# A token mixer's projections computed as three products of fp32r parts, with the weights split on GpSimd, ScalarE and VectorE

## The reference, cut to what matters

```
x    = rmsnorm(h, final_norm)                 # end of block one
xn   = rmsnorm_2(x, g_mix)
proj = xn @ w_in
sb_q, sb_k, sb_v  (512 columns each)          # stick-breaking attention, 8 heads of 64
g_q, g_k, g_v     (512 each)                  # causal conv, silu, l2norm, gated delta rule
g_z (512), g_b, g_a (4 each)                  # output gate, beta and decay
gate_sb, gate_gdn (1024 each)                 # not touched by the change
o_sb = stick_breaking_attention(sb_q, sb_k, sb_v)
o_g  = gated_delta_rule(l2norm(q), l2norm(k), v, beta, g)
```

## Time and profile before

| | |
|---|---|
| runs of the kernel before | 1817.61, 1821.5, 1824.58 us; median 1821.5 us |
| span of the profiled execution | 1818.7 us, mean granted TensorE clock 0.960 |
| busy share in that span | PE 91%, DVE 59%, ACT 31%, POOL 19% |
| two norms, from the last down projection's end to L584 | about 696.6 to 705.6 us |
| sb_v and the first projection | 711.2 to 732 us |
| four rounds | 732.8 to 789.2 us |
| channels, g_b, g_a, g_z | 789.2 to 834.1 us |
| norm sums and reciprocal | 834.1 to 851.6 us |

### The profile page before, as it was taken

One profiled execution on the slowest core, in us unless ns is written; L12 is line 12 of the kernel. 1 busy time (PEld: TensorE's weight loads), 2 busy tenths in 40 slices (PEclk: granted clock), 3 DMA queues, 4 the chain that ended last, 5 costly groups with the idle time before them and its releaser, 6 DMA issues.

```text
span 1818.7 us, 22755 instructions
## 1 busy us (share of the span) xinstructions
PE 1647.0 (91%) x7883; PEld 1171.8 (64%) x7883; DVE 1072.1 (59%) x2454; ACT 566.0 (31%) x1111; POOL 348.4 (19%) x296
## 2 busy tenths in 40 slices
PE   7999999999999998999999999798797788888877
PEld 5888999868689995884664796444343344434333
DVE  6556555546455553546444642777777777666765
ACT  2544444335344441424110431122221222222222
POOL 3550000000000000000000000454434444443540
PEclk9999999999999998999999999799999989998989
DMA  6635566323466652522405340899999999999997
GB/s 210 187 93 162 170 187 198 133 61 99 153 181 186 198 153 67 162 95 92 185 24 185 139 151 27 353 420 421 421 421 422 421 421 421 421 421 421 422 420 297
DMA packets 205769, 437.43 MB, mean 241 GB/s; under 512 B 10608, under 2 KB 136976, under 8 KB 171792
## 3 DMA queue, kind: packets, MB, share of 16 engines
q0 software_dynamic: 36864, 268.45, 35.5%
q1 hardware_dynamic: 168848, 168.20, 28.8%
HBM read 435.54 MB, written 1.05 MB: 240 GB/s over the span
## 4 chain that ended last, share of the span: by engine, by line
PE 71%; DMA 16%; DVE 8%; issue 3%; ACT 1%; SPq 0%; POOL 0%; DVEq 0%; another core or an unknown queue 0%; ACTq 0%
PE ps L553 33%; DMA OT<-in_peer_uv,IX 13%; PE ps L1438 13%; PE ps L745 6%; PE ps L1229 3%; PE ps L1086 3%; PE ps L1099 3%; PE ps L720 2%; PE ps L584 2%; DMA SLOT<-in_peer_uv,IX 2%; DVE SLOT L2761 2%; PE ps L559 1%; PE ps L629 1%; DMA SLOT<-in_fox_w_in 1%; PE ps L1178 1%
## 5 line engine op out<-in xcount | busy, mean ns | idle before, releaser
L1944 POOL DMA_INDIRECT SLOT<-in_peer_uv,IX x128 | 138.5, 1082 | 1272.3 <-DVE IX L2755 1025.2
L1438 PE MATMUL ps<-SLOT,AR 128*128 128x512 f32 x512 | 267.2, 679 | 92.9 <-ACT AR L1862 92.9
L553 PE MATMUL ps<-ARH 128*128 128x256 f32 (+1 forms) x2248 | 298.8, 285 | 0.0
L553 PEld LDWEIGHTS ps<-ARH 128*128 128x128 f32 x2248 | 285.1, 191 | 3.8 <-issue 0.5
L1438 PEld LDWEIGHTS ps<-SLOT,AR 128*128 128x128 f32 x512 | 109.5, 219 | 244.2 <-issue 131.4
L2761 DVE SCALAR_TENSOR_TENSOR SLOT<-SLOT,V 128x1024 f32<-128x1024 f32 x128 | 153.1, 1224 | 74.5 <-DMA SLOT<-in_peer_uv,IX 72.5
L2078 DVE TENSOR_TENSOR ARH<-SLOT,ARH 128x2048 fp32r<-128x2048 f32 (+1 forms) x88 | 154.1, 1756 | 50.9 <-ACT ARH L1521 34.1
L1438 PE MATMUL ps<-AR 128*128 128x512 f32 x320 | 144.2, 600 | 8.3 <-ACT AR L1862 8.3
L1856 ACT ACTIVATE AR<-AR 128x4 f32<-128x4 f32 (+1 forms) x66 | 13.6, 205 | 370.4 <-DVE SLOT L2761 184.5
L745 PE MATMUL ps<-ARH 128*128 128x512 f32 x528 | 123.8, 390 | 0.0
L1438 PEld LDWEIGHTS ps<-AR 128*128 128x128 f32 x320 | 60.3, 192 | 81.8 <-issue 64.7
(11 more groups left out here) (424 smaller groups left out, 2611.1 us busy)
## 6 DMA issues: line engine op xcount, KB each, us to landing
SLOT<-in_w_gate SPq DMA_DIRECT2D x44, 512.0 KB, 4.0
SLOT<-in_w_up SPq DMA_DIRECT2D x44, 512.0 KB, 5.3
SLOT<-in_w_down SPq DMA_DIRECT2D x44, 512.0 KB, 5.2
SLOT<-in_w_in SPq DMA_DIRECT2D x9, 2048.0 KB, 8.2
SLOT<-in_fox_w_in SPq DMA_DIRECT2D x16, 512.0 KB
SLOT<-in_w_ckv SPq DMA_DIRECT2D x4, 2048.0 KB, 8.7
XT<-in_w_pq_by_head SPq DMA_DIRECT2D x8, 1024.0 KB
SLOT<-in_w_uq_by_pair SPq DMA_DIRECT2D x8, 768.0 KB, 4.8
```

Source lines behind the costliest of these rows:

```text
L553: m = pe.matmul(outp, l, r, start=(n_ == 0), stop=(n_ == len(pairs) - 1))
L1438: m = pe.matmul(ps[:, b, :], DIAG[:, j, :], v_row(j)[:, c * 512:(c + 1) * 512], start=False, stop=closing)
L1944: pool.indirect_dma_start(PAIR[j], None, pairs, bass.IndirectOffsetOnAxis(IX[:, t, j:j + 1], 0)).then_inc(gathered[j], 16)
```

## The change

All products of `xn` with the first 3592 columns of `w_in` (all but the gates) become three fp32r matmuls. XT is kept as two parts: ACT writes the high part from PSUM (`high_norm`), DVE the low part (`low_norm`), as the feed-forward layer does. The weights are split before use:

- sb_v (now SLOT0): POOL casts and subtracts, in four quarters of two chunks each, from the moment at which the weights are there, which is during the end of `ffn(1)`. The high parts go to OTR and the upper half of SLOT1.
- the four query and key pairs (SLOT1 and SLOT2 in turn): POOL casts the high part (`sb_pair_high`, 128 x 2048), DVE subtracts (`sb_low`, 128 x 2048). The first is placed on DVE ahead of the copy of sb_v, the second behind it, the third and fourth in rounds 0 and 1, between `sb_keep` and `sb_tail`.
- the three channel tiles (slots 3, 0, 3): ACT casts halves of 128 x 2048 (`mix_columns`), POOL subtracts (`mix_low`). ACT's casts stand in rounds 1 to 3, and, for the last tile, between the copies of the second and third channel piece.
- g_b, g_a: ACT casts, POOL subtracts, both small. g_z: ACT casts two halves after the fourth channel piece, POOL subtracts two halves; PE waits for both.
- the gates' projections still use a whole XT: POOL adds the two parts (128 x 2048) once PE has started on the work after g_z (`projected`, `xt_whole`).

The loop over rounds is written out on PE, ACT and DVE. The flush of two tiny matmuls after the first projection is gone. The SP list is reordered to match. The core of the diff:

```diff
@@ PE
-            turned(H, KC)
-            pe.wait_ge(here[2], T.next(here[2], 16))
+            turned(H, KC, reader="a")
             for t in range(NT):
                 take(6 + t)
-                grown_group(ps[:, 6 + t, :], [[(cols(XT, t, k), slot(2, KC, 512)[:, k, :])] for k in range(KC)]).then_inc(full["v"][6 + t], 1)
+                for k in range(KC):
+                    if t == 0 and k % 2 == 0:
+                        evacuated(k // 2)
+                        pe.wait_ge(mix_split[0], T.next(mix_split[0]))
+                    w = (sb_high(k), low_of(0, KC, 512)[:, k, :])
+                    for n_, (l, r) in enumerate(thirds(lambda h: cols(XHL[h], t, k), lambda h: w[h])):
...
+            def sb_proj(i):
+                p = 1 + i % 2
+                pe.wait_ge(mix_split[p], T.next(mix_split[p]))
+                take(0)
+                w = (HIGH[i % 2], low_of(p, 2, KC, P))
+                for s_ in range(2):
+                    m = group(ps[:, 0, s_ * S:(s_ + 1) * S], sum((thirds(lambda h: w[h][:, s_, k, :], lambda h: XHL[h][:, k, :]) for k in range(KC)), []))
...
             def channels(s_, g, b):
+                pe.wait_ge(mix_split[s_], T.next(mix_split[s_]))
...
+            pe.wait_ge(mix_split[2], T.next(mix_split[2], 2))
...
+            pending.append(sem("projected"))
...
+            pe.wait_ge(sem("xt_whole"), 1)
             for n_ in range(2):
                 gate_part(n_, n_)
@@ ACT
+            def mix_columns(s, g):
+                if g == 0:
+                    act.wait_ge(raw_here[s], T.next(raw_here[s], 16))
+                act.copy(columns(MIX_HIGH[s], g), columns(SLOT[s], g)).then_inc(sem("mix_high"), 1)
...
+            for i in range(3):
                 sb_soft()
                 qk_copy(0.125)
+                if i:
+                    mix_columns(3, i - 1)
                 sb_probs()
...
             sb_soft()
+            mix_columns(0, 0)
             sb_probs()
             ot_copy(2, 6)
+            mix_columns(0, 1)
             ot_copy(3, 6)
...
                 signal("pre_ready")
+                if n_ == 1:
+                    mix_columns(3, 0)
+                    mix_columns(3, 1)
...
+                if n_ == 3:
+                    act.wait_ge(raw_here[2], T.next(raw_here[2], 16))
+                    for q in range(2):
+                        act.copy(MIX_HIGH[2][:, 4 * q:4 * q + 4, :], chunks(SLOT[2], q)).then_inc(sem("mix_high"), 1)
@@ POOL
+            def mix_low(s, out_, raw, high):
+                pool.wait_ge(sem("mix_high"), T.next(sem("mix_high")))
+                pool.tensor_tensor(out_, raw, high.bitcast(F32), ALU.subtract).then_inc(mix_split[s], 1)
...
+            for q in range(4):
+                for k in (2 * q, 2 * q + 1):
+                    m = pool.tensor_copy(sb_high(k), view(SLOT[0][:], KC, 512)[:, k, :])
...
+                    m = pool.tensor_tensor(view(SLOTR[0][:], KC, 512)[:, k, :], view(SLOT[0][:], KC, 512)[:, k, :], sb_high(k).bitcast(F32), ALU.subtract)
+            pool.wait_ge(sem("ffn_over"), 1)
...
+            for i in range(PAIRS // 2):
+                sb_pair_high(i)
+            for s in (3, 0, 3):
+                for g in range(2):
+                    mix_low(s, columns(SLOTR[s], g), columns(SLOT[s], g), columns(MIX_HIGH[s], g))
+            mix_low(1, ...)
+            for q in range(2):
+                mix_low(2, chunks(SLOTR[2], q), chunks(SLOT[2], q), MIX_HIGH[2][:, 4 * q:4 * q + 4, :])
+            pool.wait_ge(sem("projected"), 1)
+            pool.tensor_tensor(XT[:], XTR[:].bitcast(F32), XT2R[:].bitcast(F32), ALU.add).then_inc(sem("xt_whole"), 1)
@@ DVE
             ffn(1)
+            signal("ffn_over")
...
-            norm("mix", squared=False)
+            scaled(H, D).then_inc(sem("xs_ready"), 1)
+            low_norm(XHL[1], XHL[0], "mix")
...
+            sb_low(0)
...
+            sb_low(1)
+            for i in range(PAIRS // 2):
                 sb_scores()
                 sb_keep()
+                if i < 2:
+                    sb_low(i + 2)
                 sb_tail()
@@ SP
+            projection(0, 1024)
+            sb_pair(0)
+            sb_pair(1)
+            projection(3, 1536)
+            projection(0, 2048)
+            sb_pair(2)
+            sb_pair(3)
+            fill(1, (slot(1, KC, 8), rows(w_in, 3584, 3592)), arrival=raw_here)
+            projection(2, 3072)
+            projection(3, 2560)
```

More of the change, by code:

```diff
@@ L653, in out_part @@
                     T.add(free["v"][6 + t])
-            def qk_part(s_):
-                if s_ == 0:
-                    take(0)
-                pe.wait_ge(here[s_], T.next(here[s_], 16))
-                m = group(ps[:, 0, s_ * S:(s_ + 1) * S], ((slot(s_, KC, P)[:, k, :], XT[:, k, :]) for k in range(KC)))
-                release(s_)
-                if s_ == 1:
-                    m.then_inc(full["a"][0], 1)
-                    T.add(free["a"][0])
-            def qk_proj():
-                qk_part(0)
-                qk_part(1)
             def flip(hh):
@@ L1023, in sb_turn @@
                 T.add(free["a"][6])
-            qk_proj()
+            sb_proj(0)
             evacuated(6, 7)
-            flush()
-            assert not pending
             sb_scores(0)
-            qk_proj()
+            sb_proj(1)
             sb_sums()
             sb_mix(0)
-            assert not pending
-            with T.loop("sb", 2) as i:
-                sb_scores(i + 1)
-                qk_proj()
+            for i in range(1, 3):
+                sb_scores(i)
+                sb_proj(i + 1)
                 sb_sums()
                 sb_turn()
-                sb_mix(i + 1)
-                assert not pending
+                sb_mix(i)
             def channels(s_, g, b):
+                pe.wait_ge(mix_split[s_], T.next(mix_split[s_]))
                 take(b)
+                w = (columns(MIX_HIGH[s_], g), columns(SLOTR[s_], g))
                 for c in range(2):
-                    m = group(ps[:, b, c * S:(c + 1) * S], ((slot(s_, KC, 512)[:, k, (2 * g + c) * P:(2 * g + c + 1) * P], XT[:, k, :])
-                                                             for k in range(KC)))
+                    m = group(ps[:, b, c * S:(c + 1) * S], sum((thirds(lambda h: w[h][:, k, c * P:(c + 1) * P], lambda h: XHL[h][:, k, :]) for k in range(KC)), []))
                 m.then_inc(full["a"][b], 1)
@@ L1052, in _ @@
             sb_scores(3)
-            pe.wait_ge(here[3], T.next(here[3], 16))
             channels(3, 0, 0)
@@ L1060, in _ @@
             sb_turn()
-            for n_, s_ in ((1, 2), (2, 3)):
-                pe.wait_ge(here[s_], T.next(here[s_], 16))
+            for n_, s_ in ((1, 0), (2, 3)):
                 for g in range(2):
@@ L1067, in _ @@
                 release(s_)
-            pe.wait_ge(here[0], T.next(here[0], 16))
+            pe.wait_ge(mix_split[1], T.next(mix_split[1]))
             take(0)
             for t in range(NT):
-                m = group(ps[:, 0, 8 * t:8 * t + 8], ((cols(XT, t, k), slot(0, KC, 8)[:, k, :]) for k in range(KC)))
+                m = group(ps[:, 0, 8 * t:8 * t + 8], sum((thirds(lambda h: cols(XHL[h], t, k), lambda h: (BAH[:, k, :], low_of(1, KC, 8)[:, k, :])[h]) for k in range(KC)), []))
             m.then_inc(full["v"][0], 1)
             T.add(free["v"][0])
-            release(0)
-            row_tile(2, (6, 7), XT, reader="a")
+            release(1)
+            pe.wait_ge(mix_split[2], T.next(mix_split[2], 2))
+            for t in range(NT):
+                take(6 + t)
+                w = (MIX_HIGH[2], low_of(2, KC, 512))
+                group(ps[:, 6 + t, :], sum((thirds(lambda h: cols(XHL[h], t, k), lambda h: w[h][:, k, :]) for k in range(KC)), [])).then_inc(full["a"][6 + t], 1)
+                T.add(free["a"][6 + t])
+            release(2)
+            pending.append(sem("projected"))
             def gate_part(n_, b, ks=range(KC)):
```

79 lines of the change are left out of this document (45 added, 34 removed).

## The result

The changed kernel takes 1839.93 us (median of four runs, 1835.25 to 1841.41), the kernel before 1821.03 (median of four, measured beside it). The ratio is 1.0105, with a 95% interval of 1.009 to 1.0119: slower by 1%. The record said 1833.0, range 1816 to 1844, and gave slower a chance of 0.50.

What follows compares the result with a forecast made beforehand. PE was taken to set the rounds' pace, with DVE and ACT as long in round 1. Terms -0.2 + 3.4 + 1.6 + 0.2 + 3.7 + 3.2 = +11.9 on 1818.7 gave 1830.6, plus 2.8: 1833.4 us, range 1816 to 1844.

Steps and rivals of the forecast that it cites:

- Norms, sb_v, first projection: Norm to first projection: POOL's casts delay DVE's gain by 3.3, cheaper PE products give back 2.6 and 1.4; sum -0.2 us.
- POOL's meeting with DVE at the end of ffn(1): Before the norm: POOL's split of sb_v meets DVE's last gated pieces, +0.5 us (0 to 1.5).
- Round 0: First round: sb_low ahead of the tail +1.7, POOL's cast of pair 2 on the log terms +1.9; taken as +3.4 us.
- Round 1: Second round: sb_low(3) ahead of the tail costs +1.6 us; ACT's channel cast falls into its wait for the tail.
- Round 2: Third round: ACT's 1.86 us cast before Exp, mostly hidden by the earlier projection, +0.2 us.
- Round 3: Last round: POOL's 4.7 us subtraction goes before DVE's last log term, +4.65, less 0.95 from PE's pieces: +3.7 us.
- Channels to reciprocal: Conv and channel stretch: POOL and DVE alternate instruction by instruction, so the conv ends later and the reciprocal with it: +3.2 us.
- Whole XT: POOL's 4.7 us sum of the two XT parts beside the 12.95 us reciprocal: 0, or +3.8 if that is held.
- Rival A: Whole mixer: POOL's hold on DVE is milder or meetings are missed, +3 us, 1825; chance of 1816 to 1829: 0.33.
- Rival C: Whole mixer: POOL does not hold DVE, PE's gain counts, -6.1 us, 1815.4; chance of under 1816: 0.12.
- Rival B: DVE instructions with one SBUF input are held too: tail signals +8, 1841; with the reciprocal held, 1845; chance 0.2.
- the 15.9 that PE's arithmetic gives: All split projections: three fp32r products in place of fp32 pairs make PE's work 15.9 us cheaper, 0.9%.

Runs made afterwards that it cites:

- e3: Changed kernel, with GpSimd's pair casts moved behind the second norm's gain and scaling, and ScalarE's round 3 cast behind Exp: 1829.87 us.
- e5: Changed kernel, with the low parts of pairs 2 and 3 subtracted by GpSimd behind the log terms, not by VectorE ahead of the tail: 1833.4 us.
- w1: Changed kernel, with twelve more matmuls of 128 x 256 on PE ahead of its wait for Exp in each round: 1833.09 us.
- e4: Changed kernel, with ScalarE's casts for the channels moved behind Exp in rounds 1 and 2: 1843.71 us.
- e1: Changed kernel, with GpSimd subtracting only each chunk's first column for channels, g_b, g_a and g_z, and PE using high parts for low ones: 1824.23 us.
- b1: Kernel before, with only a GpSimd load added: eight subtractions on unused buffers from the first keep_ready on: 1870.87 us.
- g3: Changed kernel's split, GpSimd placed off VectorE's SBUF to SBUF work, ScalarE's next-pair cast before its query/key copy: 1810.5 us, 0.9924 of the kernel before.

## Why the prediction was right, and where it was off

The sign, the mechanism and the range held; the size was 6.9 us short of the measured median. Up to the reciprocal the sum had +11.9 us and the traces have +17.5 (856.07 against 838.60); the other 1.6 of the span are the last row of the table. By its own terms, with the table's rows (the first two with PE's start of the scores, 732.06 against 732.82):

- **Norms, sb_v, first projection: -0.2 on record, -0.76 measured.** The two casts did meet the gain. They took 2.84 us and not 3.3, one of them from L2035, an instruction with one SBUF input of which the record had said that no row tells. e3 shows that all 2.84 are the casts'. The first projection ran 5.8 us. The +0.5 for POOL's meeting with DVE at the end of ffn(1) can't be read: a CAST of 128 x 256 took 1.31 us there (0.29 before), but the norm began only 0.13 later, within its 2.9 from execution to execution.
- **Round 0: +3.4, measured +4.4.** Both parts are there: GpSimd's cast at 738.60 made L2436 2.24 us, and `sb_low` lies on the path (e5). VectorE's last signal of the round comes 3.2 us later than before, near the 3.4; the other 1.2 lie behind it, in PE's mix and scores at half clock (w1: 1.27).
- **Round 1: +1.6, measured +2.1.** The last signal is 1.4 later (`sb_low`), the rest is behind it; w1 gives back 0.9.
- **Round 2: +0.2, measured +2.54.** This is the term that failed. The record had ScalarE's cast "mostly hidden by the earlier projection". The projection was not earlier: at half clock it ended late, and the cast and the table load came onto the path with it. w1 gives 2.18 of it back, and in e4, with the cast behind Exp, the round is 2.9 shorter once its collision is taken off (the estimate above).
- **Round 3: +3.7, measured +4.6.** The last log term took 4.85 us, "one instruction of about 5 us" as put; e1 and e3 give back 5.3 to 5.8.
- **Channels to reciprocal: +3.2, measured +4.6.** The conv ended 39.1 us after it began, the same as by the record's sum ("some 40" in its signs), by one DVE instruction per instruction of POOL. That it agrees to a tenth is luck: POOL began 8.2 us into the conv, by the record 6.8, and was done after 19.1, by the record 21.1 (46.5 less 25.4). PE's wait came ahead of the last channel tile (2.61 us), not of g_z as put. The 1.4 us lie behind the conv, 13.7 to the reciprocal where 12.1 was reckoned: the last four norm sums, at half clock behind a wait of 2.33, took 3.14 us, where half of the 3.60 of the earlier trace rows is 1.8. That all of it is the clock wasn't tried.
- **Whole XT: 0, measured 0**: the reciprocal took 12.95 us beside it.

So the mechanism was right and its prices nearly so; what the sum lacked was that most of the waits it put on PE also halve PE's clock for a while, and that this reaches the other engines. From round 0 to the reciprocal every term came out larger than on record. Rival A (a milder hold, or missed meetings) is out by b1 and by the held instructions in each stage above. (One of its sums is slightly off: with the conv as reckoned its terms give +5.55, not +5.4.) Rival C (no hold) is out as well. Rival B was half right: instructions with one SBUF input are held in the norm and in the conv, but neither the one-column signals nor the reciprocal, so that its +8 and +3.8 us did not come. g3 shows what C would have been worth at its best: from norm to reciprocal 129.7 us, 10.1 below before, of the 15.9 that PE's arithmetic gives. Of the other 5.8, 3.4 are in rounds 0 to 2, which VectorE's and ScalarE's chain sets: three cheaper projections were to give 4.2 there and gave 0.8. Another 1.4 are g_b, g_a and g_z, 18.1 us in place of the 16.7 reckoned, at the lower clock.

## What to carry to other kernels

In this kernel GpSimd was free help only while VectorE read PSUM, ran a reciprocal, or waited. So price each GpSimd instruction at its whole length for the first SBUF to SBUF instruction of VectorE that it can meet, and look where it goes when you put it off. Work moved to the engine that was held can cost nothing (9.1 us here), since it takes the place of a wait. And when a wait is put on PE, add a lower clock behind it as a likely term, look at the clock of PE's busy stretches too, and follow who reads what PE then delivers late.
